# A transformer block with product-key experts: the experts' weights through a DRAM grid with adding DMAs in place of one-hot products

## The reference

```python
s1 = q[..., :half] @ k1.T; s2 = q[..., half:] @ k2.T      # 8 heads, 128 keys each
v1, i1 = top_k(s1, 16); v2, i2 = top_k(s2, 16)
top, pos = top_k(v1[:, None] + v2[None, :], 16)           # of 256 sums
idx = i1 * 128 + i2 at pos                                # one of 16384 experts
g = softmax(top)
act = gelu(sum_d u_tab[idx] * h) * g                      # 8 * 16 experts a token
out = sum over (head, k) of act * v_tab[idx]
```

## Time and profile before

| | us |
|---|---|
| median of 3 runs | 1830.88 (1829.05 to 1831.99) |
| profiled execution | 1830.48, its span 1828.5 |
| UP, 32 blocks | 559 to 721 |
| MID, 32 blocks | 721 to 884 |
| ROUTE, 64 blocks | 884 to 1226.6 |
| DOWN, 128 blocks | 1230 to 1814 |

### The profile page before, as it was taken

One profiled execution on the slowest core, in us unless ns is written; L12 is line 12 of the kernel. 1 busy time (PEld: TensorE's weight loads), 2 busy tenths in 40 slices (PEclk: granted clock), 3 DMA queues, 4 the chain that ended last, 5 costly groups with the idle time before them and its releaser, 6 DMA issues.

```text
span 1828.5 us, 29128 instructions
## 1 busy us (share of the span) xinstructions
PE 1796.5 (98%) x9970; PEld 1573.4 (86%) x9970; DVE 1586.2 (87%) x2605; ACT 825.1 (45%) x1190; POOL 207.8 (11%) x193
## 2 busy tenths in 40 slices
PE   7999999999999999999999999999999999999998
PEld 6888888445999999999999999997888888888886
DVE  4669899966778999999999999998888888888887
ACT  3011222302635555333566666664555555554544
POOL 1000000110000000111122121121111111111110
PEclk9999999999999999999999999999999999999999
DMA  9998666798686677998999999999999999999994
GB/s 381 420 421 344 261 253 253 296 422 357 240 321 260 225 251 254 366 337 322 340 347 371 362 359 364 363 357 373 385 361 375 367 375 364 368 365 376 364 376 202
DMA packets 98051, 616.94 MB, mean 337 GB/s; under 512 B 13218, under 2 KB 21954, under 8 KB 26434
## 3 DMA queue, kind: packets, MB, share of 16 engines
q1 hardware_dynamic: 61314, 414.22, 58.8%
q0 software_dynamic: 25408, 184.58, 26.6%
q10 hardware_dynamic: 11266, 17.32, 2.6%
HBM read 599.22 MB, written 16.79 MB: 337 GB/s over the span
## 4 chain that ended last, share of the span: by engine, by line
PE 77%; DVE 10%; DMA 8%; issue 3%; ACT 1%; DVEq 0%; SPq 0%; ACTq 0%
PE ps L1329 30%; PE ps L963 15%; PE ps L970 9%; PE ps L1014 6%; PE ps L1130 5%; DMA raw<-in_w_ada 5%; PE ps L1184 4%; PE ps L1281 2%; PE ps L1025 2%; DVE big L1411 2%; DVE raw L1436 2%; DVE w_low L1389 1%; DMA big<-in_w_gate_f 1%; DVE big L1492 1%; DMA raw<-in_peer_v 1%
## 5 line engine op out<-in xcount | busy, mean ns | idle before, releaser
L676 ACT ACTIVATE w_hi<-raw 128x1024 fp32r<-128x1024 f32 x520 | 551.4, 1061 | 491.4 <-PE ps L1329 240.4
L1389 DVE TENSOR_TENSOR w_low<-raw,w_hi 128x1024 fp32r<-128x1024 f32 x520 | 632.8, 1222 | 90.0 <-ACT w_hi L676 83.3
L1329 PE MATMUL ps<-w_hi,a 128*128 128x512 f32 x1536 | 390.1, 389 | 0.8 <-ACT w_hi L676 0.5
L963 PE MATMUL ps<-a,w_hi 128*128 128x384 f32 x1856 | 374.1, 342 | 0.9 <-issue 0.8
L1329 PEld LDWEIGHTS ps<-w_hi,a 128*128 128x128 f32 x1536 | 288.2, 188 | 61.3 <-ACT w_hi L676 0.9
L963 PEld LDWEIGHTS ps<-a,w_hi 128*128 128x128 f32 x1856 | 316.0, 189 | 1.9 <-issue 1.7
L1329 PE MATMUL ps<-w_low,a 128*128 128x512 f32 x1024 | 274.2, 390 | 1.6 <-DVE w_low L1389 1.6
L970 PEld LDWEIGHTS ps<-a,w_low 128*128 128x128 f32 x1856 | 238.0, 191 | 8.0 <-DVE w_low L1389 7.5
L970 PE MATMUL ps<-a,w_low 128*128 128x192 f32 x1856 | 241.3, 272 | 3.2 <-DVE w_low L1389 2.9
L1329 PEld LDWEIGHTS ps<-w_low,a 128*128 128x128 f32 x1024 | 191.8, 188 | 42.6 <-DVE w_low L1389 3.0
L1436 DVE CUSTOM_DVE_ANT_0 raw<-raw,big 128x2048 f32<-128x2048 f32 x64 | 146.2, 2290 | 61.4 <-DMA raw<-in_w_ada 61.4
(11 more groups left out here) (229 smaller groups left out, 1692.1 us busy)
## 6 DMA issues: line engine op xcount, KB each, us to landing
raw<-in_peer_u SPq DMA_DIRECT2D x128, 1024.0 KB
raw<-in_peer_v SPq DMA_DIRECT2D x128, 1024.0 KB
early<-in_w_front SPq DMA_DIRECT2D x56, 1024.0 KB, 9.1
raw<-in_w_ada POOLq DMA_DIRECT2D x48, 1024.0 KB, 8.5
raw<-in_w_ada SPq DMA_DIRECT2D x32, 1024.0 KB, 12.6
raw<-in_peer_wq SPq DMA_DIRECT2D x16, 1024.0 KB
big<-in_w_gate_f SPq DMA_DIRECT2D x16, 1024.0 KB, 7.0
gel_saved<-stage ACTq DMA_DIRECT2D x64, 192.0 KB
```

The lines of the kernel that those rows point to most:

```text
L676: act.activation(w_hi[:, h % 2, :], raw[:, s % RING, :], ACT.Copy).then_inc(hi_ready, 1)
L963: done = pe.matmul(ps[:, b % 2, 0:2 * TD].rearrange("p (m t) -> p m t", m=2), w_hi[:, ph.nth(j) % 2, k * P:(k + 1) * P], a_pair[:, kc, :, ...
L1329: done = pe.matmul(ps[:, 4 * tt + 2 * (j % 2) + n, :], a, w[:, n * 512:(n + 1) * 512], start=i is None and blk == 0 and m in (0, 2), stop= ...
L1389: dve.tensor_tensor(w_low[:, s % RING, :], raw[:, s % RING, :], w_hi[:, h % 2, :].bitcast(F32), ALU.subtract).then_inc(lo_ready, 1)
```

## The change

- Experts of a token are written by address. A DRAM tensor `weights` (32 groups x 128 x 4x192 floats, 12.6 MB) is zeroed in UP by 16 DMAs of ScalarE's queue. VectorE works out each choice's place in it (`tile_gates`, once for each token tile). GpSimd issues 192 indirect DMAs (`put_weights`), each adding 128 weights of four bytes: 64 for the 64 dense tokens of the second tile (two halves of the choices side by side in the partitions), 128 for the first tile. `PUTS_BEHIND` says how many follow each gather: 8 after row 1, 4 after rows 2 to 15, none after 16 to 18, then 4, 3, 3, 3 in turn. The first put of a head (every 8th in the first 64, every 16th then) waits until all puts before it have landed.
- Masks, one-hot products, their copies, the turning of the choice and their semaphores go.
- ROUTE becomes two stages, THIRD and LAST, of 32 blocks each. The order of the u_tab blocks changes (`U_ORDER`), so that the gelu of each block can be written directly to its place in `routed` over memory that is free by then; the gelu outputs' way to DRAM and back goes.
- In DOWN SP's queue reads groups of `weights` in place of gelu outputs, with the same sizes; the first two stand behind the first block's load and wait for all puts.
- The exponent and the gates of the second tile are worked out in MID's first iteration, those of the first tile in THIRD's. Two small DMAs for `row_gate` move there with four more for the puts' data.

```diff
+PH_UP = Phase(PH_WQ, EXPERT_BLOCKS // 32, 16, groups=tuple(range(22, 30)))
+PH_MID = Phase(PH_UP, EXPERT_BLOCKS // 32, 16, plain=(1, 3, 7, 9, 11, 15), groups=(30, 31, 4, 11, 12, 13, 14, 15))
+PH_THIRD = Phase(PH_MID, EXPERT_BLOCKS // 32, 16, groups=(5, 6, 7, 8, 9, 10, 16, 17))
+PH_LAST = Phase(PH_THIRD, EXPERT_BLOCKS // 32, 16, groups=(0, 1, 2, 3, 18, 19, 20, 21))
+PH_DOWN = Phase(PH_LAST, EXPERT_BLOCKS // 8, 16)
+U_ORDER = [4 * g + i for ph in (PH_UP, PH_MID, PH_THIRD, PH_LAST) for i in range(4) for g in ph.groups]
...
+PUTS_SECOND, PUTS_FIRST = PEER_HEADS * TOPK // 2, PEER_HEADS * TOPK
+PUTS = PUTS_SECOND + PUTS_FIRST
+PUTS_BEHIND = [0, 8] + [4] * (DOT_ROWS[PH_THIRD] - 2) + [0] * 3 + [4, 3, 3, 3] * 12
...
@@ SP
+            def weights_first(j, i):
+
+                if j == 1:
+                    sp.wait_ge(weights_put, 16 * PUTS)
+                    weights_group(0, None)
+                    weights_group(1, None)
...
@@ GpSimd
+            def put_weights(n):
+
+                head_first = n % (TOPK // 2) == 0 if n < PUTS_SECOND else n % TOPK == 0
+                if n == 0:
+                    gp.wait_ge(weights_zero, 16 * GROUPS // 2)
+                    gp.wait_ge(put_in, 16 * 2 * SLICES)
+                elif n == PUTS_SECOND:
+                    gp.wait_ge(sel_ready, 2)
+                if head_first and n:
+                    gp.wait_ge(weights_put, 16 * n)
+                gp.indirect_dma_start(weight_elements, bass.IndirectOffsetOnAxis(ap=put_at[:, n:n + 1], axis=0),
+                                      put_gate[:, n:n + 1], None, compute_op=ALU.add).then_inc(weights_put, 16)
...
                 gather(n, u_rows, got[n % 2], row_in[n % 2])
+                for m in range(PUTS_AT[n], PUTS_AT[n + 1]):
+                    put_weights(m)
...
@@ ScalarE
-                act.activation(stage[:, b % 4, :], ps[:, b0 % 2, 0:TD], ACT.Gelu).then_inc(gemm_evac, 1)
+                act.activation(routed_v[:, bass.ds(place, 1), :].rearrange("p o t -> p (o t)"),
+                               ps[:, (ph.block + n) % 2, 0:TD], ACT.Gelu).then_inc(gemm_evac, 1)
...
+            def clear_weights(q, i):
+
+                dst = weights[bass.ds(at(i, 8, 2 * q), 2)].rearrange("g p n -> p g n")
+                zeros = weights_in[0][:, :, :].rearrange("p a t -> p (a t)")
+                act.dma_start(dst, zeros[:, None, :].to_broadcast([P, 2, 4 * TD])).then_inc(weights_zero, 16)
...
+                if j == 5:
                     act.wait_ge(sel_ready, 1)
                     for n in range(SLICES):
...
+                        picks_now = slice(n * TOPK // 2, (n + 1) * TOPK // 2)
+                        for place, src in ((put_gate, gates[0:TS, 0:PEER_HEADS, picks_now]),
+                                           (put_at, put_second[0:TS, :, picks_now])):
+                            act.dma_start(place[n * TS:(n + 1) * TS, 0:PUTS_SECOND]
+                                          .rearrange("p (h k) -> p h k", k=TOPK // 2), src).then_inc(put_in, 16)
...
@@ TensorE
-            def weights(g, i):
...
-            for n in range(PH_ROUTE.blocks):
-                product(PH_ROUTE, n, None, ahead=ahead_first)
-            with pe.Fori(1, PH_ROUTE.n) as i:
-                for n in range(PH_ROUTE.blocks):
-                    product(PH_ROUTE, n, i, ahead=ahead_route)
+            for ph in (PH_THIRD, PH_LAST):
+                for n in range(ph.blocks):
+                    product(ph, n, None)
+                with pe.Fori(1, ph.n) as i:
+                    for n in range(ph.blocks):
+                        product(ph, n, i)
...
@@ VectorE
-            def make_masks(g, i):
...
+                if ph is PH_MID and i is None and q == 0:
+                    tile_gates(0, gates[:, 0:PEER_HEADS], put_second)
...
+            def tile_gates(n, out_gate, out_at):
+
+                rows = slice(n * PEER_HEADS, (n + 1) * PEER_HEADS)
+                dve.wait_ge(gate_exp, n + 1)
+                sel_link(dve.tensor_reduce(gate_sum[:, rows], gates[:, rows], AXX, ALU.add))
+                sel_link(dve.reciprocal(gate_sum[:, rows], gate_sum[:, rows]))
...
+                sel_link(dve.tensor_copy(put_second, idx1[:, rows]))
+                sel_link(dve.tensor_scalar(put_second, put_second, 3, None, ALU.bitwise_and))
+                dve.tensor_copy(expert_f, put_second)
+                places = put_f.rearrange("p (h k) -> p h k", k=TOPK)
+                sel_link(dve.tensor_scalar(places, idx1[:, rows], float(KEYS * TD), token[:, 1 - n:2 - n], ALU.mult, ALU.add))
+                sel_link(dve.scalar_tensor_tensor(places, idx2[:, rows], float(4 * TD), places, ALU.mult, ALU.add))
+                sel_link(dve.scalar_tensor_tensor(places, expert_f, float(-(KEYS - 1) * TD), places, ALU.mult, ALU.add))
+                dve.tensor_copy(out_at, places).then_inc(sel_ready, 1)
```

More of the change, by code:

```diff
@@ L46, with __init__ @@
 class Phase:
-    def __init__(self, before, n, per, plain=()):
-        self.n, self.per, self.plain = n, per, plain
+    def __init__(self, before, n, per, plain=(), groups=()):
+        self.n, self.per, self.plain, self.before, self.groups = n, per, plain, before, groups
         self.s = before.s_end if before else 0
@@ L789, in put_weights, with gelu @@
-            def put_weights(g, i):
-                act.wait_ge(oh_used, at(i, 6, g + 1))
-                act.activation(routed_by_token[:, bass.ds(at(i, 24, 4 * g), 4), :],
-                               ps[:, 2 + g % 6, :].rearrange("p (a b) -> p a b", a=4), ACT.Copy).then_inc(w_evac, 1)
-            def route(j, i, put_at):
-                for g in range(6):
-                    if put_at[g] == j:
-                        put_weights(g, i)
+            def gelu(ph, n, i):
+                act.wait_ge(summed, at(i, ph.blocks, ph.block + n - B_UP + 1))
+                if n >= 0:
+                    place = at(i, 1, 4 * ph.groups[n])
+                elif i is None:
+                    place = 4 * ph.before.groups[n] + ph.before.n - 1
+                else:
+                    place = at(i, 1, 4 * ph.groups[n] - 1)
+                act.activation(routed_v[:, bass.ds(place, 1), :].rearrange("p o t -> p (o t)"),
+                               ps[:, (ph.block + n) % 2, 0:TD], ACT.Gelu).then_inc(gemm_evac, 1)
@@ L809, in up_unit @@
                 if j % 2 == 0:
-                    gelu(ph.block + m - 2, i, per)
-                elif m % 2 and not (first and m == 1):
-                    save_pair(ph.block - B_UP + m - 2, i, per)
+                    gelu(ph, m - 2, i)
+                elif m % 2 and ph is PH_UP:
+                    clear_weights(m // 2, i)
             for j in range(PH_UP.per):
+                if j == 3:
+                    act.wait_ge(zeros_made, 1)
+                    clear_weights(0, None)
+                if j == 10:
+                    act.wait_ge(gate_f_sum, 1)
                 if j >= 2:
@@ L842, in _ @@
                                       expert_u[P - TS:P, n * ROWS:(n + 1) * ROWS]).then_inc(row_ix_in, 16)
-            with act.Fori(1, PH_MID.n) as i:
-                for j in range(PH_MID.per):
-                    up_unit(PH_MID, j, i)
-            for j in range(PH_ROUTE.per):
-                up_unit(PH_ROUTE, j, None)
-                if j == 1:
-                    act.wait_ge(gate_in, 1)
-                    act.activation(gates, gates, ACT.Exp).then_inc(gate_exp, 1)
-                if j == 3:
+                    act.wait_ge(x2_saved, 16)
+                if j == 5:
                     act.wait_ge(sel_ready, 1)
@@ L1405, in dots_at @@
                 if n == 0 and half == 0:
-                    if i is not None or row0 != ROW_MID:
-                        before = PH_MID.n if row0 == ROW_ROUTE else 0
+                    if i is not None or before:
                         dve.wait_ge(dots_put, at(i, 1, before))
```

249 lines of the change are left out of this document (102 added, 147 removed).

## The result

The changed kernel takes **1946.1 us** (median; 1939.4 to 1948.0) against 1830.0 for the kernel before on the same chip, a ratio of 1.0625 (1.0611 to 1.0640). It is slower by 116 us. The forecast was 1845 with a range from 1800 to 1925.

What follows compares the result with a forecast made beforehand. TensorE was taken as today's bound, with GpSimd's queue next: its 43 us saving is paid back, leaving +5 us in the rewritten stage and +9 in MID on 1830.48, plus the median's 0.4, 1845 us; range 1800 to 1925.

Steps and rivals of the forecast that it cites:

- What bounds the kernel, and what goes: Rewritten stages: TensorE bounds, busy 341.45 of 342.60 us; 48 groups of one-hot products go, saving 43.2 us.
- The price of a put: GpSimd, last stages: a put costs 1.26 us like a mean gather, plus a 0.30 gap, 1.56 us.
- The row arithmetic: Last stages: one gather and 3.25 puts take GpSimd 6.77 us a row against TensorE's 6.27; 320.7 us before drains.
- The drains: Last stages: seven GpSimd waits at heads until earlier puts land, 3.8 us each, adding 27 us; stage 347.7 us.
- MID's first iteration: MID's start: small VectorE steps, six small DMAs and eight puts delay gather 2 to near 749; +9 us.
- Later in MID free: MID after its first iteration: a row has about 10 us against 7.1 of GpSimd, so puts cost nothing.
- The DMA engines: Rewritten stages: 14.7 MB an iteration at 421 GB/s take 34.9 of 37.6 us, leaving 22 us in the stage.
- A: Rewritten stages and MID: puts cost the shortest gather, 1.24 us with the gap; only drains remain; 1808 us; chance 0.31.
- C: Everything hides: puts under 1 us and drains ending at once give the full saving, 1789 us; chance 0.05.
- Rival B2: Rewritten stages: DMA engines become the bound, 67 ns per four-byte addition; 1881 us, 1958 at twice that price; chance 0.09.
- B: GpSimd: the addition doubles issuing work, 2.5 us a put; 1957 us, 1900 half way from the forecast; chance 0.12.
- Everything else at nothing: Zero fills, grid loads in DOWN, gelu's direct write and the other small changes cost nothing; DOWN's 584 us unchanged.

Runs made afterwards that it cites:

- run 8: Changed kernel without puts and their data, each gather for the dots bringing half a row: 1784.5 us, ratio 0.9747.
- run 3: Changed kernel with each put adding to places of its own, so no head waits for earlier puts: 1910.3 us, ratio 1.0426.
- run 10: run 9 with 4, 3, 3, 3, 3 puts behind the last stages' gathers, so each head's first put directly follows a gather: 1921.4 us, ratio 1.0490.
- run 7: Changed kernel with the first 64 puts alone, the 128 of the third and last stages left out: 1846.3 us, ratio 1.0075.
- run 2: Changed kernel without all 192 puts and without the four small DMAs that bring their data: 1811.9 us, ratio 0.9898.
- run 5: Changed kernel with the 192 puts written as plain stores instead of additions: 1874.3 us, ratio 1.0235.
- run 1: Changed kernel with all 192 puts left out, their small data DMAs kept: 1818.0 us, ratio 0.9922.
- run 9: Changed kernel with VectorE first laying out the second tile's gates and places by halves, so small DMAs read 256-byte runs: 1933.1 us, ratio 1.0559.

## Why the prediction was wrong, step by step

*What bounds the kernel, and what goes: right.* TensorE's saving is 43 us where nothing else is late; run 8 ends 46 us under the kernel before, with eight blocks at 37.65 us.

*The price of a put: the step that failed.* The prediction took 1.26 us from the mean gather of two stages, plus 0.30, and said that indices cost the same in a put as in a gather. Indices do: a store takes 0.954 us at the shortest, a gather 0.94. What I left at nothing, for want of a row, is the addition: 1.536, or 0.58 more than a store. That is the whole miss of 0.57. The rest up to the mean of 1.83 is VectorE, 0.29, and the forecast had it: 1.26 is 0.32 over the shortest gather. An order of time shows VectorE's part, GpSimd first, then VectorE in the same microseconds:

```profile
1007.79 2.56 POOL L490 DMA_INDIRECT weights<-sel  x1 [0.30 <-issue]
1010.66 2.08 POOL L490 DMA_INDIRECT weights<-sel  x1 [0.31 <-issue]
1013.05 1.54 POOL L490 DMA_INDIRECT weights<-sel  x1 [0.30 <-issue]
```

```profile
1007.68 1.23 DVE L1364 TENSOR_TENSOR w_low<-raw,w_hi 128x1024 fp32r<-128x1024 f32 x1
1008.83 1.22 DVE L1385 CUSTOM_DVE_ANT_0 big<-big 128x1024 f32<-128x1024 f32 x1
...
1010.09 1.23 DVE L1364 TENSOR_TENSOR w_low<-raw,w_hi 128x1024 fp32r<-128x1024 f32 x1
```

The first put begins 0.11 us after a subtraction and ends at 1010.35, 1.44 us after that subtraction's end (1008.91); the second ends 1.42 us after the end of the next one (1011.32); the third begins while VectorE is idle and takes 1.54. A put that begins inside a subtraction waits for its end and then needs nearly its whole time; the half dot that follows at 1008.83 doesn't lengthen it again. Over the whole trace, worked out from its order of time, the 94 puts that begin inside a subtraction or a half dot take 2.08 us on average, and the 75 that begin with VectorE idle 1.55; those few that begin inside VectorE's search steps (MAX8, FIND_INDEX8, MATCH_REPLACE8) take 1.54 to 1.57. No run varied VectorE's work, so this part is read from the trace alone. The Trainium skill's "SBUF — State Buffer" (SBUF: two separate sides) says that a VectorE step with two inputs in SBUF holds a port pair against a GpSimd operation that reads SBUF, for the whole instruction; the trace agrees. The reverse isn't seen: a half dot that began at 1013.53, inside the third put, took its usual 1.23.

With 1.83 for 1.26 the prediction's own sum gives 128x0.57 = 73 us more, 347.7+73 = 421, against 420.5 measured. The row arithmetic was right and one term of it was mis-sized, and that term is multiplied by 128. That the two agree to a microsecond is partly luck: the seven drains took 31.6 us where the sum has 27, and the rows without puts made up for it. Of the 101 us between forecast and result some 73 lie here; MID has the other part, 42 us in the place of 9. I took the mean within a bounded span of 1.24 to 2.2 and called the costly half unlikely (0.12) on the ground that the indices are as many.

*The drains: right in kind and size in the last stages, left out in MID.* Seven, forecast at 3.8 us each, 27 in all; measured 31.6. MID has seven more, each right behind a gather's issue, which the prediction had at nothing: 17.2 us of GpSimd's waits (48.8 in all). Run 3 takes 36 away with both, and run 10 shows that a drain inside a row, behind the gather, costs more than one ahead of the row's first put.

*MID's first iteration: right in mechanism, too small.* Gather 2, at 739.84 in the earlier trace rows, was forecast near 749. It came at 761.69:

```profile
745.62 2.27 POOL L490 DMA_INDIRECT weights<-sel  x1 [16.20 <-DMA sel<-big]
...
761.69 1.00 POOL L477 DMA_INDIRECT big<-in_u_rows,row_ix  x1 [0.31 <-issue]
```

Eight puts took 16.1 us, not 11.4, and their data landed some 6 to 9 us later than thought (745.6, not 737 to 740), since the six small DMAs held ScalarE's queue 13 us and not 3.8. I had priced them by DMAs of 64 long runs; the four for the puts read 512 runs of 32 bytes each. TensorE stood still for ten of those microseconds.

*"Later in MID free": wrong by the same price.* Four puts at 1.77+0.30 and a gather at 1.26+0.30 (the means in MID's window) are 9.8 us of the 10.2 that a row has, not 7.1, and a drain every second row adds 1.2 a row, to 11. Nothing was in hand when the first rows came late. By run 7, MID's puts cost 28 us in all.

*The DMA engines: half right.* They are no bound in the changed kernel (0.84). But as the floor under the rows the 421 GB/s of the front part was the wrong row to take; gathers and table blocks together reach 359 to 387 in run 2's busiest stretches. The 34.9 us per iteration should have been 38 to 41, and the floor of a row 6.3 to 6.8 us, not 6.27. Rivals A (1808) and C (1789) rested on the lower floor: with every put gone the kernel takes 1818, and without the puts' data 1812. The row to use stood there: 0.94 busy at 358 GB/s, so the engines had room for 6% more, not for 18.

*Rival B2, packets.* GpSimd's DMA queue holds this on the page of the changed kernel, and then on that of run 5 (packets, MB, share of 16 engines):

```profile
q0 software_dynamic: 53056, 184.69, 27.8%
```

```profile
q0 software_dynamic: 31552, 184.69, 26.3%
```

In the kernel before it was 25408 packets (26.6% of 1828.5 us). An added put sends 144 packets (27648/192), as counted in the prediction; a stored one 32. The share says 541 us of each engine against 486 before, 55 more for 1728 packets, or 31 ns each, between the two ends I had put (7 and 67); this is an estimate, as it gives the whole rise of the queue's share to the puts. It stays under the time that GpSimd takes. The decision between forecast and B went by GpSimd's price alone.

*Everything else at nothing:* DOWN at 582 us, UP unchanged, the grid's zeroing and its loads hidden. Right.

The ledger of the 116 us: -19 for what the lost products give with the rows as they are (run 2), +6 for the small DMAs (run 1 less run 2), +28 for MID's puts, +96 for those of the last stages, and 4 or 5 that the parts don't hold. The 24 us that run 2 lacks of the full 43 are in the first of these. Of the 128 us of the puts, the addition is 72 (run 5) and the drains 36 (run 3); these two overlap, since a dearer put lengthens the drain too.

## What to carry to other kernels

A queue that is idle today is no room for work whose price no row shows: when one unknown price is multiplied by a hundred, the range must follow its upper end, and one small run of that instruction alone settles it before the kernel is rewritten. Before counting a saving, work out the next bound from the busiest row of the same stage, not from another stage's best rate. Instructions that must come in the order of a shared queue (gathers behind puts) carry every delay to the consumers of both, so put the drains where nothing urgent stands behind them.

## What the runs showed of the hardware that was not expected

- An indirect DMA that adds takes GpSimd 1.54 us at the shortest for 128 indices, a plain one 0.95; an adding one of 64 indices takes hardly less (1.40). It sends a packet per element (144 with the semaphores' 16), a store 32.
- Four DMAs of 16 KB, each in 512 runs of 32 bytes, held ScalarE's queue for 10 us (1.71+8.28); each in 64 runs of 256 bytes, for 2.7 (run 9).
- After ten idle microseconds TensorE ran eight products in 2.93 us where 1.58 was usual, with the granted clock at 0.50, the lower of its two levels. The first row is TensorE in MID's first iteration, the second the window around it:

```profile
742.04 2.93 PE L988 MATMUL ps<-a,w_hi 128*128 128x384 f32 x8 [9.94 <-ACT big L799]
```

```profile
742.00:745.20 3.20, 3.16 (x11) 3.16 (x12) 3.10 (x5) 1.16 (x2) 0.00 (x0) 0.50 0.04 9
```

- Beside gathers the DMA engines moved 359 to 387 GB/s in stretches of 20 us in which they were 0.98 to 1.00 busy (run 2), where the front part of the kernel before had 421 at 1.01. The Trainium skill's "SBUF — State Buffer" (A bandwidth-pool intuition that's wrong) gives some 358 GB/s between HBM and a core; the means of the long stages agree (358 to 365), the busiest stretches and the front part go over it.
